# Norms by halves of 512 columns, the last MLP blocks by token tile, the first tile ahead in two projections, and the mixer's squares on ACT

## The reference, cut to what matters

```python
# first_block: layer 0 differential attention, layer 1 block attention
for layer in range(2):
    mix = diff_attention(h, ...) if layer == 0 else moba_attention(h, ...)
    h = layer_norm(ALPHA * h + mix, ln1_g[layer], ln1_b[layer])
    h = layer_norm(ALPHA * h + squared_relu_mlp(h, w_up[layer], w_down[layer]),
                   ln2_g[layer], ln2_b[layer])
# second_block
mod = silu(c) @ w_ada + b_ada            # sh1, sc1, g1, sh2, sc2, g2
u = rmsnorm(h, norm1) * (1 + sc1) + sh1
h = h + g1 * token_mixer(u, w_in, ...)   # retention and latent attention
u = rmsnorm(h, norm2) * (1 + sc2) + sh2
h = h + g2 * hier_moe(u, ...)            # 32 experts, top 2 in one group
out = rmsnorm(h, final_norm)
```

## Time and profile before

| | |
|---|---|
| median of 3 runs | 1335.26 us (1333.67 to 1336.22) |
| the profiled execution | 1335.65 us, its span 1333.6 us |
| PE busy | 1218.1 us, 91% |
| DVE busy | 748.0 us, 56% |
| ACT busy | 515.8 us, 39% |
| granted PE clock, mean | 0.942 |
| HBM read | 281.87 MB, 213 GB/s over the span |

### The profile page before, as it was taken

How to read it: one execution, slowest core, us unless ns; L and a number is a source line. 1 busy time by engine, 2 the same in 40 slices (tenths; PEclk the granted TensorE clock), 3 DMA queues, 4 the chain that set the end, 5 groups by cost and what they waited for, 6 DMA issues and landing times. The chain is left out here.

```text
span 1333.6 us, 18671 instructions
## 1 busy us (share of the span) xinstructions
PE 1218.1 (91%) x7419; PEld 1005.8 (75%) x7419; DVE 748.0 (56%) x1252; ACT 515.8 (39%) x852; POOL 53.0 (4%) x94
## 2 busy tenths in 40 slices
PE   7998799999899889999789999999888799999994
PEld 5886699998699689999687778787666566666663
DVE  3577677778666677777863336453565622222224
ACT  4576444443455444444343323345432222222221
POOL 5000000000000000000000000000000000000000
PEclk9999799999899989999889779999988699999998
DMA  9943388777353339887453205355374299999992
GB/s 276 249 162 110 106 280 283 278 278 270 122 184 106 127 129 332 288 279 283 134 141 94 95 32 173 117 175 173 126 272 138 93 367 367 367 365 365 365 365 84
DMA packets 175748, 285.02 MB, mean 214 GB/s; under 512 B 11549, under 2 KB 137754, under 8 KB 175296
## 3 DMA queue, kind: packets, MB, share of 16 engines
q1 hardware_dynamic: 165616, 248.76, 55.9%
q0 software_dynamic: 10064, 35.32, 8.2%
HBM read 281.87 MB, written 2.20 MB: 213 GB/s over the span
## 5 line engine op out<-in xcount | busy, mean ns | idle before, releaser
L1613 DVE TENSOR_TENSOR w_lo<-ring,w_hi 128x1024 fp32r<-128x1024 f32 (+1 forms) x272 | 320.2, 1211 | 131.9 <-ACT w_hi L1219 124.4
L1219 ACT ACTIVATE w_hi<-ring 128x1024 fp32r<-128x1024 f32 (+1 forms) x272 | 277.9, 1050 | 169.2 <-PE acc L578 152.6
L576 PE MATMUL pp<-x_hi,w_hi 128*128 128x256 f32 x896 | 263.3, 294 | 8.8 <-DVE x_lo L1603 6.8
L577 PE MATMUL pp<-x_lo,w_hi 128*128 128x256 f32 x896 | 259.2, 289 | 0.0
L578 PE MATMUL pp<-x_hi,w_lo 128*128 128x256 f32 x896 | 258.8, 289 | 0.0
L576 PEld LDWEIGHTS pp<-x_hi,w_hi 128*128 128x128 f32 x896 | 177.5, 198 | 17.2 <-issue 8.1
L577 PEld LDWEIGHTS pp<-x_lo,w_hi 128*128 128x128 f32 x896 | 177.7, 198 | 1.4 <-issue 0.2
L578 PEld LDWEIGHTS pp<-x_hi,w_lo 128*128 128x128 f32 x896 | 177.5, 198 | 0.0
L576 PE MATMUL acc<-w_hi,x_hi 128*128 128x512 f32 (+2 forms) x384 | 154.9, 403 | 13.4 <-DVE x_lo L1603 6.8
L577 PE MATMUL acc<-w_lo,x_hi 128*128 128x512 f32 (+2 forms) x384 | 151.3, 394 | 0.0
L578 PE MATMUL acc<-w_hi,x_lo 128*128 128x512 f32 (+2 forms) x384 | 150.8, 393 | 0.0
(11 more groups left out here) (342 smaller groups left out, 1725.7 us busy)
## 6 DMA issues: line engine op xcount, KB each, us to landing
ring<-in_w_up_dram SPq DMA_DIRECT2D x32, 1024.0 KB, 5.4
ring<-in_w_down_dram SPq DMA_DIRECT2D x32, 1024.0 KB, 6.9
ring<-in_w_dram SPq DMA_DIRECT2D x32, 1024.0 KB, 12.6
stage<-in_w_ada_dram POOLq DMA_DIRECT2D x48, 512.0 KB, 6.4
ring<-in_w_in_dram SPq DMA_DIRECT2D x24, 1024.0 KB, 5.0
big<-in_w_dram SPq DMA_DIRECT2D x24, 1024.0 KB, 11.2
ring<-in_w_in_a_dram SPq DMA_DIRECT2D x12, 1024.0 KB, 14.4
ring<-in_w_kv_shared_dram SPq DMA_DIRECT2D x8, 1024.0 KB, 6.1
```

Of the source, the lines that this page charges most:

```text
L576: pe.matmul(out, lhs[0], rhs[0], start=start, stop=False)
L577: pe.matmul(out, lhs[0], rhs[1], start=False, stop=False)
L1219: act.activation(shaped(high_half(b, k), raw), raw, ACT.Copy).then_inc(S["hi_ready"], 1)
L1613: dve.tensor_tensor(shaped(low_half(b, k), raw), raw, shaped(high_half(b, k), raw), ALU.subtract).then_inc(S["lo_ready"], 1)
```

## The change

Five edits, in the order of the program:

1. After an attention, the last output block finishes one bank after the other (tile 0 half 0, tile 0 half 1, tile 1 half 0, tile 1 half 1), and `part_ready` tells each. DVE adds and takes statistics by halves. In three of the four norms half of tile 1 is summed before tile 0 is normalised (or, after MLP 1, before the statistics of its mean square).
2. The first up block of an MLP waits for the third split, and for the fourth from its second quarter on.
3. Blocks 30 and 31 of an MLP are interleaved: 30 for both tiles in its first half, 30's second half for tile 0, 31 for tile 0, 30's second half for tile 1, 31 for tile 1.
4. The value projection of attention 1 and the latent projection (`tile_first_out`) begin with 12 products of tile 0 as soon as its first split is there; tile 1's transposes follow, then the second weight block for tile 0, then both blocks for tile 1. After MLP 0, DVE does the first split ahead of tile 1's statistics.
5. After MLP 1 the sum of squares is an ACT instruction with an accumulator, and ACT also scales tile 0's rows; DVE scales tile 1's.

```diff
+            def tile_first_out(b, turn, cuts=(0, 512, 1024), before=lambda i, j: None):
...
+                pe.wait_ge(S["x_split"], base + 1)
+                for i in range(2):
+                    for j in range(4):
+                        if j % 2 == 0:
+                            half_ready(b + i, j // 2)
+                        part(i, j, 0)
+                    if i == 0:
+                        turn()
+                pe.wait_ge(S["x_split"], base + 3)
+                for i in range(2):
+                    for j in range(4):
+                        last = part(i, j, 1)
+                        if j % 2 == 1:
+                            last.then_inc(S["half_used"], 1)
+                pe.wait_ge(S["x_split"], base + 4)
+                for i in range(2, 4):
...
-                tokens_out(b, before=vectors)
+                if layer == 0:
+                    tokens_out(b, before=vectors)
+                else:
+                    norm_tile(1, 0)
+                    tile_first_out(b, lambda: norm_tile(1, 1))
...
-                out_block(3, [0]).then_inc(S["tile_ready"], 1)
-                out_block(3, [1])
...
+                    for half in range(2):
+                        for k in range(2):
+                            if q == 0 and half == 0:
+                                half_ready(b + 15, k)
+                            last = product(acc[:, 2 * q + half, :], x_parts(6 + k, slice(q * 128, (q + 1) * 128)),
+                                           w_parts(b + 15, k, slice(512 * half, 512 * half + 512)),
+                                           start=False, stop=(k == 1))
+                            if q == 1 and half == 1:
+                                last.then_inc(S["half_used"], 1)
+                        if q == 0 or half == 0:
+                            last.then_inc(S["part_ready"], 1)
...
+                def before(j):
+                    if j < 2:
+                        pe.wait_ge(S["x_split"], base + 3 + j)
...
+                v = PAIRS - 2
+                pe.wait_ge(S["hid_ready"], PAIRS * layer + v + 1)
+                half_ready(b + 30, 0)
+                down_half(v, 0, 0)
+                down_half(v, 0, 1).then_inc(S["half_used"], 1)
+                half_ready(b + 30, 1)
+                down_half(v, 1, 0)
                 pe.wait_ge(S["hid_ready"], PAIRS * (layer + 1))
...
+                for f in range(2):
+                    half_ready(b + 31, f)
+                for half in range(2):
+                    for f in range(2):
+                        last = down_part(v + 1, 2 * f + half, 0)
+                    last.then_inc(S["part_ready"], 1)
+                down_half(v, 1, 1).then_inc(S["half_used"], 1)
+                for half in range(2):
+                    for f in range(2):
+                        last = down_part(v + 1, 2 * f + half, 1)
+                        if half == 1:
+                            last.then_inc(S["half_used"], 1)
+                    if half == 0:
+                        last.then_inc(S["part_ready"], 1)
...
+            pe.wait_ge(S["r_row0"], 1)
+            tile_to_feature_major(o_tm, 0)
+
+            def turn_second():
+                pe.wait_ge(S["r_out"], 1)
+                tile_to_feature_major(o_tm, 1)
+
+            tile_first_out(B_C, turn_second, cuts=(0, 384, 704))
...
+            mixer_squares(0)
             mixer_root(0)
+            act.wait_ge(S["r_rstd"], 1)
+            act.activation(o_tm[:, 0, :], h_tm[:, 0, :], ACT.Identity, scale=rstd[:, 2:3]).then_inc(S["r_row0"], 1)
             norm_root(3, 1)
             act.wait_ge(S["modc_done"], 1)
-            mixer_input(0, 1)
+            mixer_input(0)
+            mixer_squares(1)
             mixer_root(1)
+            mixer_input(1)
             mixer_input(0, 1)
...
+            def sum_part(i, b, q, half):
+
+                if q == 1 and half == 1:
+                    used(b)
+                else:
+                    dve.wait_ge(S["part_ready"], 3 * i + 2 * q + half + 1)
+                cols = slice(512 * half, 512 * half + 512)
+                link(dve.scalar_tensor_tensor(o_tm[:, q, cols], h_tm[:, q, cols], ALPHA, acc[:, 2 * q + half, :],
+                                              ALU.mult, ALU.add))
+                return dve.bn_stats(st6[:, q, half, :], o_tm[:, q, cols])
...
+                sum_tile(i, b, 0)
+                tile_stat(0)
+                if i != 1:
+                    sum_part(i, b, 1, 0)
+                    normalise(0)
+                else:
+                    normalise(0)
+                    sum_part(i, b, 1, 0)
+                link(sum_part(i, b, 1, 1))
+                if i == 1:
+                    split_input(1)
+                tile_stat(1)
                 normalise(1)
...
+            sum_tile(3, b, 0)
+            tile_stat(0)
             last_norm(0)
...
+            sum_part(3, b, 1, 0)
+            mixer_stat(0)
+            link(sum_part(3, b, 1, 1))
+            tile_stat(1)
             last_norm(1)
...
+            split_input(1)
+            mixer_stat(1)
+            dve.wait_ge(S["r_rstd"], 2)
+            dve.tensor_scalar(o_tm[:, 1, :], h_tm[:, 1, :], rstd[:, 3:4], None, ALU.mult).then_inc(S["r_out"], 1)
+            split_input(3)
             low(B_C + 1, n=5)
```

More of the change, by code:

```diff
@@ L624, in tokens_out, with part @@
                             last.then_inc(S["half_used"], 1)
+            def tile_first_out(b, turn, cuts=(0, 512, 1024), before=lambda i, j: None):
+                def part(i, j, q):
+                    k, half = divmod(j, 2)
+                    kt = 2 * i + k
+                    n = cuts[half + 1] - cuts[half]
+                    return product(acc[:, 2 * q + half, 0:n], x_parts(kt, slice(q * 128, (q + 1) * 128)),
+                                   w_parts(b + i, k, slice(cuts[half], cuts[half + 1])),
+                                   start=(kt == 0), stop=(kt == 7))
+                base = inputs[0]
+                inputs[0] += 4
+                pe.wait_ge(S["x_split"], base + 1)
[14 more added lines that the diff above has]
+                for i in range(2, 4):
+                    for j in range(4):
+                        before(i, j)
+                        if j % 2 == 0:
+                            half_ready(b + i, j // 2)
+                        for q in range(QT):
+                            last = part(i, j, q)
+                        if j % 2 == 1:
+                            last.then_inc(S["half_used"], 1)
             def features_out(b, bank, before=lambda j: None):
@@ L773, in attention, with norm_tile @@
                 input_split()
-                out_block(3, [0]).then_inc(S["tile_ready"], 1)
-                out_block(3, [1])
-            def norm_transposes(i):
                 for q in range(QT):
-                    pe.wait_ge(S["ln_out"], QT * i + q + 1)
                     for half in range(2):
-                        transposes([(128 * j, o_tm[:, q, (4 * half + j) * 128:(4 * half + j + 1) * 128])
-                                    for j in range(4)])
-                input_split()
+                        for k in range(2):
[8 more added lines that the diff above has]
+                            last.then_inc(S["part_ready"], 1)
+            def norm_tile(i, q):
+                pe.wait_ge(S["ln_out"], QT * i + q + 1)
+                tile_to_feature_major(o_tm, q)
             def mlp(layer):
                 b = B_MLP[layer]
+                base = inputs[0]
+                inputs[0] += 4
+                def before(j):
+                    if j < 2:
+                        pe.wait_ge(S["x_split"], base + 3 + j)
                 def up(v):
@@ L839, in _ @@
                 attention(layer)
-                norm_transposes(2 * layer)
+                for q in range(QT):
+                    norm_tile(2 * layer, q)
                 mlp(layer)
-                if layer == 0:
-                    norm_transposes(1)
             pe.wait_ge(S["ada_done"], 1)
@@ L862, in mod_rows @@
                         .then_inc(S["mod_mm"], 1)
-            for q in range(QT):
-                pe.wait_ge(S["r_out"], q + 1)
-                for half in range(2):
-                    transposes([(128 * j, o_tm[:, q, (4 * half + j) * 128:(4 * half + j + 1) * 128])
-                                for j in range(4)])
-            input_split()
-            tokens_out(B_C, cuts=(0, 384, 704))
+            pe.wait_ge(S["r_row0"], 1)
[4 more added lines that the diff above has]
+            tile_first_out(B_C, turn_second, cuts=(0, 384, 704))
             def rqk(i):
@@ L1592, in split_plain, with split_part, split_input @@
                     last.then_inc(S["tp_split"], 1)
[L1594 to L1604 removed]
+            def split_part():
+                n = inputs[0]
+                g, (q, half) = input_groups[n], divmod(n % 4, 2)
+                inputs[0] += 1
+                dve.wait_ge(S["tp_done"], turns_done(g))
```

(8 more changed lines are left out.)

117 lines of the change are left out of this document (47 added, 70 removed).

## The result

| | before | after |
|---|---|---|
| median, runs of one comparison | 1335.41 us (1333.67 to 1336.22, 4 runs) | 1346.89 us (1345.23 to 1347.72, 4 runs) |
| ratio after / before | | 1.0086, 95% interval 1.0069 to 1.0104 |
| profiled execution, span | 1335.65, 1333.6 us | 1345.23, 1343.2 us |
| PE, DVE, ACT busy | 1218.1, 748.0, 515.8 us | 1226.8, 744.2, 519.3 us |
| granted PE clock, mean | 0.942 | 0.938 |

The change makes the kernel slower, as predicted, but by about three times as much: +11.5 us where +3.8 was forecast, and outside the range.

What follows compares the result with a forecast made beforehand. PE, busy 91% of 1333.6 us, was taken to bound the kernel, its long waits lying in the norms. Terms -3.2 + 5.9 + 1.1 = +3.8 gave a median of 1339.1 us, range 1335.0 to 1342.6.

Steps and rivals of the forecast that it cites:

- priced stages: Norms after both attentions, MLP 0's end and MLP 1's end: -3.2 + 5.9 + 1.1 = +3.8 us.
- Norms after the attentions: Twice: the MLP's first block waits for split 3 only, so PE starts earlier; -1.6 us each, -3.2 for both.
- Tail of the MLPs: Last down blocks: PE stands 0.95 us for w_lo; the first sum comes 3.1 us later after MLP 0.
- MLP 0's end in all: Tail, norm and value projection after MLP 0: PE goes on at 350.85, +5.9 us, ends +4.0 and +6.4.
- MLP 1's end: Tail, norm and latent projection after MLP 1: +3.0 - 1.9 = +1.1 us, ends -0.5 and +1.7.
- Squares on ACT: Norm after MLP 1: taken at 1.25 us, buying back the tail's 2.5 us and nothing more.
- I take the same loss as before: Granted clock at the four restarts after the norms: shifted but not removed, so no change in its loss.
- a delay passes on whole: Behind the priced places PE waits little and DVE's and SP's work follows PE, so delays reach the end in full.
- rival of a longer low clock: Low clock of 5.8 us at every restart and in two early runs of 12 products: +4.0, 1343.1 us; chance 0.15.
- The clock comes back in the early run: Rival: tile 0's 12 early products raise the clock and it holds until PE goes on; -0.7 to -2.1 us; chance 0.12.
- stated marks: Trace signs: PE waits for w_lo near 324 and 646.4, late first sums, a gap of about 5 us ending with w_lo.
- two limits in absolute positions: After MLP 0: prediction wrong if the first sum starts before 329 or PE goes on before 348.

Runs made afterwards that it cites:

- e1: Kernel before with only the interleaved order of the last two down blocks on PE at both MLP ends; 1338.99 us against 1334.98, ratio 1.0035.
- e6: Kernel before with 12 early products of tile 0 at the latent projection alone; 1338.16 us, ratio 1.0026.
- d4: Changed kernel with the old MLP tail and without the 12 early products at the value and latent projections; 1331.38 us, ratio 0.9972.
- c1: Changed kernel measured again, nothing altered; 1341.02 us against 1334.74, ratio 1.0054.
- e5: Changed kernel with the next stage's second w_lo half after tile 0's normalisation and the second weight block made before tile 1's splits; 1321.51 us, ratio 0.9907.
- e7: Changed kernel with only the next stage's second w_lo half moved behind tile 0's normalisation on DVE; 1334.94 us, ratio 1.0011.
- d1: Kernel before with 8 extra harmless matmuls (0.96 us) near 698 us, to shift what follows; 1339.98 us, ratio 1.0035.
- d2: Changed kernel with 19 extra harmless matmuls (2.3 us) near 698 us; 1339.52 us, ratio 1.0034.
- c3: Changed kernel unaltered, a single run for its trace; 1346.54 us.
- c4: Changed kernel unaltered, another single run for its trace; 1343.36 us.

## Why the prediction was wrong

The sign and the mechanism of the priced stages were right: they sum to +3.4 where +3.8 was forecast. What failed is the step that put everything behind them at nothing.

- **Norms after the attentions**, -1.6 each: PE's first product behind them comes 1.9 us earlier in the first (148.65 to 145.58, of which 1.2 was there before the norm) and 1.8 in the second. The clock then adds -0.9 in the first, where it rose after 3.7 us instead of 5.82, and +0.6 in the second. Right.
- **Tail of the MLPs**, a stall of 0.95 and a sum 3.1 us later: the stall shows as 0.86 idle. The sum starts at 327.66 against 328.35, and since the whole kernel stood 4.0 us earlier by then, that is 3.3 later. Alone (e1) the tail costs 3.4 and 3.0. Right.
- **MLP 0's end in all**, +5.9 with 6.4 as its end: +6.1 in the first trace, +6.1 to +7.2 in the five others of this kernel. In these the restart ran 3.4 to 4.4 us at the lower clock, against 3.41 before, besides the early run at a mean of 0.56 (4.82 us). Right, and a little small over all.
- **MLP 1's end**, +1.1: +1.4. Squares on ACT cost what was taken, 1.25 (timeline after MLP 1):

```profile
660.15 1.06 ACT L1490 ACTIVATE o_tm<-h_tm 128x1024 f32<-128x1024 f32 x1 [2.30 <-DVE h_tm L2005]
661.12 0.19 ACT L1490 ACTIVATION_READ_ACCUMULATOR o_tm<-h_tm 128x1 f32 x1
```

  The runs e1, e6 and d4 have +3.0 (tail), +0.5 (early run) and -2.7 (squares and half sums) here, 0.9 together. Right.
- **"I take the same loss as before"** for the clock and **"a delay passes on whole"** behind these places: these are the steps that failed. The first spoke only of the four restarts, and the second put block 2 at nothing, where the trace has +7.4. The rest of the kernel has lighter stretches (near 706, 748, 851, 941, 968 and 1303) in which the clock is granted or not by where they fall, and each costs 1.4 to 1.7 us. The traces of the study put block 2 anywhere from -3.0 to +7.4 us, and those of the changed kernel from +4.0 to +7.4, so the +3.8 needed a term there of that width, and the range a good 7 us above it. The rival of a longer low clock looked at the right cause in the wrong place. That c1's median, 1341.02, lies inside the stated range is luck: the forecast had no term for block 2, and what c1's shorter runs lack is open.
- **The clock comes back in the early run** was half right. It rose at the end of the early run after MLP 0 (0.56 over 336.18 to 341.00) and behind that after MLP 1, and by the time the long products ran it was gone (0.54 and 0.50), as the prediction argued against this rival. In e5, without the gap, it stays.
- The stated marks held: PE waits for w_lo in both tails, the sum stands behind a waiting w_lo, a gap of 4.94 us ends with a w_lo. The two limits in absolute positions were both undercut, PE at 346.98 (limit 348) and the first sum at 327.66 (limit 329). They were badly set: the kernel stood 4.0 us earlier by then, and as distances from the last block both came out as forecast. One sum of the working is off: its terms' upper ends, -2.4 + 6.4 + 1.7, bring the author's case to 1341.0, not 1341.2, which changes nothing.
- The Trainium skill, page "TensorE: Matmul & The Clock Gate", says in the section "Step-by-step: what each phase is for" (the prediction named another section of the page) that matmuls stay in program order. Tile 1's rows were ready at 336.90 + 0.81 = 337.7 and its transposes began at 341.00, behind all 12 products. The trace agrees.

## What to carry to other kernels

When PE's order is changed, the lists of the engines that feed it must be changed with it: a weight half that waits for a release stood ahead of work that was ready, and moving it by a few places took the change's loss away (e7), and with the second block made in the gap as well a kernel 0.5 to 0.9% slower became one 0.9% faster (e5). Before pricing a change of a few us, look through the whole trace for stretches where the granted clock is below 1.00 or has nearly no dense work under it, and put them into the range: they move with the program. A difference under 1% that rests on four runs of one comparison wants a second one, and a shift by harmless work (d1, d2) shows how much of it can be position.

## What the runs showed of the hardware

- The clock rose at the end of the early run and stayed at 1.00 through 5.98 us with 1.04 us of matmuls, then fell when the products went on (0.54 over 3.72 us). The raised clock under that gap was lost; without the gap (e5) the long products went on at 1.00.
- The same 27 matmuls near 706 took 5.61 us at 1.00 and 7.29 at a mean of 0.77, with PE busy throughout in both.
- One kernel, run again, differed by 8 us (1339.86 to 1347.72 over its timed runs) and so did the kernel before (1331.76 to 1339.69). What two traces of one kernel show of it (c3 and c4, 3.0 us) lay in the granted clock: PE's idle time in the two windows is alike, 1.97 and 1.5 us.
